# Samples' sums in four groups of eight rows up to the output, in a decoder layer with 32 experts

## The reference, cut to what matters

```python
h = h + mix
x = rmsnorm(h, norm_ffn)
gates, top_idx = softmax(top_k(x @ w_router + b_router, 4))
# per expert e: act = swiglu(x[rows] @ w_up[e] + b_up[e]); y = act @ w_down[e] + b_down[e]
h = h + einsum('tk,tkd->td', gates, y)
y_prompt, y_sample = rmsnorm(h[:256], norm_final), rmsnorm(h[256:], norm_final)
# rmsnorm(x, g) = x * rsqrt(mean(x * x) + 1e-6) * g
```

## Time and profile before

| | |
|---|---|
| median of three runs | 1089.74 us (1089.80, 1089.74, 1088.01) |
| the profiled execution, its own time | 1090.6 us |
| its span in the profile | 1088.8 us |
| busy in the span: PE, DVE, ACT, POOL | 1066.5, 361.5, 152.7, 12.1 us |
| moved by the DMA engines | 431.47 MB, 396 GB/s on average |
| granted clock of TensorE, mean | 0.995 |

### The profile page before, as it was taken

One profiled execution on the slowest core, in us unless ns is written; L12 is line 12 of the kernel. 1 busy time (PEld: TensorE's weight loads), 2 busy tenths in 40 slices (PEclk: granted clock), 3 DMA queues, 4 the chain that ended last, 5 costly groups with the idle time before them and its releaser, 6 DMA issues.

```text
span 1088.8 us, 13132 instructions
## 1 busy us (share of the span) xinstructions
PE 1066.5 (98%) x5662; PEld 446.4 (41%) x5663; DVE 361.5 (33%) x571; ACT 152.7 (14%) x302; POOL 12.1 (1%) x28
## 2 busy tenths in 40 slices
PE   8999999999999999999999999999999999999997
PEld 6888664333333333333333333333333333333332
DVE  3466534322222222222222222222332222232234
ACT  1121144111101111111111110111111011011113
POOL 1000000000000000000000000000000000000002
PEclk9999998999999999999999999999999999999999
DMA  9875948999999999999999999999999999999994
GB/s 293 305 266 205 393 170 329 407 428 430 433 427 434 427 430 433 432 429 431 428 434 430 429 435 426 432 428 432 433 430 433 428 430 434 422 427 427 427 409 172
DMA packets 40907, 431.47 MB, mean 396 GB/s; under 512 B 4456, under 2 KB 19852, under 8 KB 25104
## 3 DMA queue, kind: packets, MB, share of 16 engines
q1 hardware_dynamic: 40240, 430.41, 94.4%
q10 hardware_dynamic: 608, 0.20, 0.1%
HBM read 427.00 MB, written 3.48 MB: 395 GB/s over the span
## 4 chain that ended last, share of the span: by engine, by line
PE 80%; DMA 18%; DVE 0%; issue 0%; ACT 0%; POOLq 0%; DVEq 0%; POOL 0%; ACTq 0%
PE bank L999 35%; PE bank L1018 14%; DMA ring_all<-in_w_up 14%; PE bank L681 9%; PE bank L1063 5%; DMA ring_all<-in_w_down 4%; PE bank L973 4%; PE bank L1010 2%; PE bank L791 2%; PE bank L981 2%; PE bank L991 1%; PE bank L643 1%; PE bank L1056 1%; PE bank L1075 1%; PE bank L799 1%; PE bank L1101 1%
## 5 line engine op out<-in xcount | busy, mean ns | idle before, releaser
L999 PE MATMUL bank<-ring_all,work 128*64 128x512 f32 x2048 | 486.3, 602 | 7.9 <-DMA ring_all<-in_w_up 7.9
L999 PEld LDWEIGHTS bank<-ring_all,work 128*64 128x64 f32 x2048 | 135.0, 136 | 258.3 <-issue 248.8
L1018 PE MATMUL bank<-ring_all,work 128*64 128x512 f32 x992 | 225.3, 596 | 1.0 <-DMA ring_all<-in_w_down 1.0
L1827 DVE TENSOR_TENSOR h_tok<-h_tok,bank 128x1024 f32<-128x1024 f32 (+1 forms) x67 | 81.7, 1220 | 237.1 <-PE bank L1063 231.3
L1018 PEld LDWEIGHTS bank<-ring_all,work 128*64 128x64 f32 x992 | 68.5, 137 | 129.8 <-issue 128.8
L681 PE MATMUL bank<-work,ring_all 128*128 128x264 f32 x384 | 86.9, 387 | 0.0
L1797 DVE TENSOR_TENSOR work<-bank,bias_up 128x1024 f32<-128x1024 f32 x32 | 39.1, 1223 | 124.9 <-PE bank L1010 124.9
L681 PEld LDWEIGHTS bank<-work,ring_all 128*128 128x128 f32 x384 | 72.4, 190 | 12.4 <-DMA ring_all<-in_w_in 0.3
L1063 PE MATMUL bank<-work 64*128 64x512 f32 (+1 forms) x268 | 75.1, 637 | 0.0
L1814 DVE TENSOR_TENSOR work<-work 128x512 f32<-128x512 f32 x32 | 22.2, 692 | 108.6 <-ACT work L1403 108.5
L1387 ACT ACTIVATE work<-bank 128x264 f32<-128x264 f32 x32 | 12.5, 391 | 315.9 <-PE bank L991 315.9
(11 more groups left out here) (233 smaller groups left out, 546.3 us busy)
## 6 DMA issues: line engine op xcount, KB each, us to landing
ring_all<-in_w_up SPq DMA_DIRECT2D x48, 4096.0 KB, 33.2
ring_all<-in_w_down SPq DMA_DIRECT2D x24, 4096.0 KB, 34.2
ring_all<-in_w_up SPq DMA_DIRECT2D x30, 2048.0 KB, 37.9
ring_all<-in_w_down SPq DMA_DIRECT2D x13, 2048.0 KB, 39.8
ring_all<-in_w_in SPq DMA_DIRECT2D x13, 1024.0 KB, 5.1
ring_all<-in_w_down SPq DMA_DIRECT2D x6, 1024.0 KB, 22.0
ring_all<-in_w_out SPq DMA_DIRECT2D x4, 1024.0 KB, 11.8
ring_all<-in_w_up SPq DMA_DIRECT2D x4, 1024.0 KB, 5.8
```

The costliest lines, as they stand in the source:

```text
L999: mm = pe.matmul(bank[half * CAP:(half + 1) * CAP, up_bank(n) + b, :].rearrange("q (k p) -> q p k", k=KT), x, src[:, half * FF + b * 512:h ...
L1018: mm = pe.matmul(bank[half * CAP:(half + 1) * CAP, Y, :], av[:, 2 * i + k, :], src[:, k * D + half * 512:k * D + (half + 1) * 512], start= ...
L1827: tt(rows, rows, bank[0:m, b:b + 2, :], ALU.add).then_inc(comb_added, 1)
```

## The change

The samples' sums stay in the four groups of `sums` up to the output.

- All experts and the bias use the small pieces for c = 2. At expert 0, eight more products with the identity start the accumulation with the samples' rows of `h_tok`. The joining at expert 26 is gone.
- `sums` keeps its place, so norm_final moves into slot 6 of the ring (`late`), after chunk 186 of 192 has been used. SP loads, behind the last weights, a 0/1 matrix `same_row` (64 KB, row i and row j have a one where i and j are equal modulo 32), norm_final for the prompt, and norm_final once more for each of the four groups (`g_fold`): six transfers for one, with a semaphore of their own that POOL and PE wait for.
- The last combines, adds and squares of half 1 go in the order samples, tile 0, tile 1. For the samples they are over 128 partitions x 128 columns.
- The sums of squares of a sample's four groups are joined by two products of one column with `same_row` on PE, behind PE's register load and branch. DVE adds epsilon from PSUM, and POOL takes the samples' power together with tile 0's; tile 1 has its own.
- DVE scales tile 0, then all 256 columns of `sums` in one operation, then tile 1. ACT scales the two prompt tiles alone, and POOL multiplies two tiles where it did three.
- The samples are stored by four transfers of 8 rows x 2 pieces x 512 bytes, two issued by SP between the stores of tile 0 and tile 1, two by ACT behind its last row.

```diff
-            gt = lay(6304, T)[P - E:P]
-            g_fin = lay(5280, D)
+            gt = lay(6304, SEQ + 32)[P - E:P]
+            late = ring_all[:, LATE % RING, :]
+            g_fin = late[:, 0:D]
+            g_fold = late[:, D:D + 2 * P].rearrange("p (a b) -> p a b", a=2)
+            same_row = late[:, D + 2 * P:D + 3 * P]
-            weighted = [h_rows[:, 0:512], h_rows[:, 512:1024], xg[0:NS, :]]
+            weighted = [h_rows[:, 0:512], h_rows[:, 512:1024]]
...
-            FOLD = 26
+            LASTS = (2, 0, 1)
+            SCALE = (7, 6, 8)
...
+            last_sums = [(0, 0), (0, 1), (0, 2)] + [(1, c) for c in LASTS]
...
+            def y_folded(g):
+                return y_sample.rearrange("b s (n g t) -> g (b s) n t", n=2, g=4)[g]
...
-                sp.wait_ge(comb_psum, CT * (FOLD + 1))
+                sp.wait_ge(mm_done, LATE + 1)
+                sp.dma_start(same_row, c_square[:, 8, :]).then_inc(fin_in, 16)
                 sp.dma_start(g_fin[:], norm_final.rearrange("(a d) -> a d", a=1)
-                             .partition_broadcast(P)[:, 0, :]).then_inc(late_in, 16)
+                             .partition_broadcast(P)[:, 0, :]).then_inc(fin_in, 16)
+                for g in range(4):
+                    sp.dma_start(g_fold[32 * g:32 * g + NS], norm_final.rearrange("(a n g t) -> g a n t", a=1, n=2, g=4)[g]
+                                 .partition_broadcast(NS)[:, 0]).then_inc(fin_in, 16)
...
                 each_overflow(sp, greatest_load(sp), overflow)
-                for c in range(2):
-                    sp.wait_ge(fin_ready, c + 1)
-                    sp.wait_ge(fin_rows, c + 1)
-                    sp.dma_start(y_prompt[0, c * P:(c + 1) * P, :], h_tok[:, c, :]).then_inc(stored, 16)
+                sp.wait_ge(fin_ready, 1)
+                sp.wait_ge(fin_rows, 1)
+                sp.dma_start(y_prompt[0, 0:P, :], h_tok[:, 0, :]).then_inc(stored, 16)
+                sp.wait_ge(fin_ready, 2)
+                for g in range(2):
+                    sp.dma_start(y_folded(g), sums[32 * g:32 * g + NS]).then_inc(stored, 16)
                 sp.wait_ge(fin_ready, 3)
-                sp.wait_ge(fin_rows, 3)
-                sp.dma_start(y_sample.rearrange("b s d -> (b s) d"), h_tok[0:NS, 2, :]).then_inc(stored, 16)
-                sp.wait_ge(stored, 48)
+                sp.wait_ge(fin_rows, 2)
+                sp.dma_start(y_prompt[0, P:2 * P, :], h_tok[:, 1, :]).then_inc(stored, 16)
+                sp.wait_ge(stored, 96)
...
-                pool.wait_ge(late_in, 32)
-                for c in range(CT):
+                pool.wait_ge(fin_in, 96)
+                for c in range(2):
                     pool.wait_ge(comb_added, CT * (E - 1) + c + 1)
-                def last_root(c0, c1, i):
-                    pool.wait_ge(fin_ssq, c1)
-                    pool.tensor_tensor(st[:, 6 + c0:6 + c1], st[:, c0:c1], st[:, 3 + c0:3 + c1], ALU.add).then_inc(fin_chain, 1)
-                    pool.wait_ge(fin_chain, i + 1)
-                    pool.tensor_tensor(st[:, 6 + c0:6 + c1], st[:, 6 + c0:6 + c1],
-                                       minus_half[:].broadcast_to([P, c1 - c0]), ALU.pow).then_inc(fin_scale, 1)
-
-                pool.wait_ge(fin_eps, 1)
-                last_root(0, 1, 0)
-                last_root(1, CT, 1)
+                    pool.tensor_tensor(weighted[c], h_tok[:, c, 0:512], g_fin[:, 0:512], ALU.mult).then_inc(fin_weighted, 1)
+
+                def last_root(c, cols):
+                    at = SCALE[c]
+                    pool.tensor_tensor(st[:, at:at + 1], st[:, c:c + 1], st[:, 3 + c:4 + c], ALU.add).then_inc(fin_chain, 1)
+                    pool.wait_ge(fin_chain, c + 1)
+                    pool.tensor_tensor(st[:, at:at + cols], st[:, at:at + cols],
+                                       minus_half[:].broadcast_to([P, cols]), ALU.pow).then_inc(fin_scale, 1)
+
+                pool.wait_ge(fin_eps, 2)
+                pool.wait_ge(fin_ssq, 2)
+                last_root(0, 2)
+                pool.wait_ge(fin_ssq, 3)
+                last_root(1, 1)
...
-                    if c == 2 and isinstance(n, int) and n < FOLD:
+                    slot = n % 2 if isinstance(n, int) else 0
+                    if c == 2:
+                        if isinstance(n, int) and n == 0:
+                            for g in range(4):
+                                for half in range(2):
+                                    pe.matmul(bank[32 * g:32 * g + 32, C + half, 0:P], ident[0:NS, 0:32],
+                                              h_tok[0:NS, 2, half * 512 + g * P:half * 512 + (g + 1) * P], start=True, stop=False)
                         for g in range(4):
                             for half in range(2):
                                 at = slice(half * CAP, (half + 1) * CAP)
-                                mm = pe.matmul(bank[32 * g:32 * g + 32, C + half, 0:P], spread[at, n % 2, t0:t0 + 32],
-                                               y_rows[at, g * P:(g + 1) * P], start=True, stop=True)
+                                mm = pe.matmul(bank[32 * g:32 * g + 32, C + half, 0:P], spread[at, slot, t0:t0 + 32],
+                                               y_rows[at, g * P:(g + 1) * P], start=(not isinstance(n, int) or n > 0), stop=True)
                         mm.then_inc(comb_psum, 1)
                         return
-                    fold = c == 2 and isinstance(n, int) and n == FOLD
                     for half in range(2):
                         at = slice(half * CAP, (half + 1) * CAP)
-                        mm = pe.matmul(bank[0:m, at_bank + half, :], spread[at, n % 2 if isinstance(n, int) else 0, t0:t0 + m],
-                                       y_rows[at, :], start=True, stop=not fold)
-                    if fold:
-                        for half in range(2):
-                            for g in range(4):
-                                mm = pe.matmul(bank[0:m, C + half, g * P:(g + 1) * P], ident[:, 32 * g:32 * g + m],
-                                               sums[:, half, :], start=False, stop=(g == 3))
+                        mm = pe.matmul(bank[:, at_bank + half, :], spread[at, slot, t0:t0 + m],
+                                       y_rows[at, :], start=True, stop=True)
                     mm.then_inc(comb_psum, 1)
...
-                def combine_last(p, c):
-
+                def combine_last(i):
+
+                    p, c = last_sums[i]
                     t0, m = TOK[c]
-                    i = CT + CT * p + c
-                    pe.wait_ge(comb_added, CT * (E - 2) + i - 1)
-                    if c == 0:
+                    b = CL[(i + 1) % 2]
+                    pe.wait_ge(comb_added, CT * (E - 1) + i - 1)
+                    if i % CT == 0:
                         pe.wait_ge(y_copied, E + p)
                         pe.wait_ge(spread_copied, E)
-                    for half in range(2):
-                        at = slice(half * CAP, (half + 1) * CAP)
-                        mm = pe.matmul(bank[0:m, CL[i % 2] + half, 0:256], spread[at, (E - 1) % 2, t0:t0 + m],
-                                       y_rows[at, p * 256:(p + 1) * 256], start=True, stop=True)
+                    if c == 2:
+                        for g in (0, 2, 1, 3):
+                            at = slice(g // 2 * CAP, (g // 2 + 1) * CAP)
+                            mm = pe.matmul(bank[32 * g:32 * g + 32, b, 0:P], spread[at, (E - 1) % 2, t0:t0 + 32],
+                                           y_rows[at, p * 256 + g % 2 * P:p * 256 + (g % 2 + 1) * P], start=True, stop=True)
+                    else:
+                        for half in range(2):
+                            at = slice(half * CAP, (half + 1) * CAP)
+                            mm = pe.matmul(bank[:, b + half, 0:256], spread[at, (E - 1) % 2, t0:t0 + m],
+                                           y_rows[at, p * 256:(p + 1) * 256], start=True, stop=True)
                     mm.then_inc(comb_psum, 1)
...
-                                       start=True, stop=True)
+                        if c == 2:
+                            for g in range(4):
+                                mm = pe.matmul(bank[32 * g:32 * g + 32, C + half, 0:P], gt[:, t0:t0 + 32],
+                                               b_down_sb[:, half * 512 + g * P:half * 512 + (g + 1) * P], start=True, stop=True)
+                        else:
+                            mm = pe.matmul(bank[:, C + half, :], gt[:, t0:t0 + m], b_down_sb[:, half * 512:(half + 1) * 512],
...
                 each_overflow(pe, greatest_load(pe), overflow)
+                pe.wait_ge(fin_in, 96)
+                pe.wait_ge(fin_part, CT)
+                pe.wait_ge(fin_ssq, 1)
+                pe.matmul(bank[:, X, 0:1], same_row, st[:, 2:3], start=True, stop=False)
+                pe.matmul(bank[:, X, 0:1], same_row, st[:, 5:6], start=False, stop=True).then_inc(sel_psum, 1)
...
-                    n = TOK[c][1]
```

(66 more changed lines are left out.)

61 lines of the change are left out of this document (32 added, 29 removed).

## The result

| | before | after |
|---|---|---|
| median of ten runs | 1089.03 us (1088.01 to 1092.26) | 1092.72 us (1091.01 to 1094.22) |
| the profiled execution, its own time | 1090.6 us | 1091.75 us |
| its span | 1088.8 us | 1089.9 us |

The ratio is 1.0031, with a 95% interval from 1.0023 to 1.0039. The change costs about 3.4 us (2.5 to 4.2 by the interval). The forecast was no change, and the time lies above the range.

What follows compares the result with a forecast made beforehand. Up to 1058 us PE and the DMA transfers were taken as nearly equal streams, transfers landing last; time saved before counted 0, the tail's terms summed to +0.1 us on the 1089.74 median: forecast 1089.8, range 1087.9 to 1091.2.

Steps and rivals of the forecast that it cites:

- Steps (1) to (3): PE before 1058 us: eight more products (0.38), smaller bias product, small combines saving 4.16 us; all behind transfers, counted 0.
- rival A: PE is the bound up to 1058 us, so 4.16 us come through: 1085.6; chance 0.05, partial form 0.03.
- The named sign: Waits for ring_all grow by about 4 us between 952 and 1058, PE still passing its weights near 1058.
- Step (4): Samples' combine of expert 30 on PE, behind the last transfer PE waits for: 0.96 becomes 0.38, -0.58 us.
- Step (5): Last combines, adds and squares in the new order: squares end at 1081.9, chain 1.3 us shorter.
- Step (6): Samples' scale in series over PE, DVE, POOL behind PE's branch: first scale 0.2 us later (1082.8), second 0.7 earlier (1083.6).
- rival B: Late samples' path and SP's queue: 1090.7; with PE's code fetched, 1092 to 1093; fetch form shares 0.07 with late six transfers.
- The second scale: POOL's power for the second prompt block: 0.27 + 0.55 after the first scale, at 1083.6, 0.7 us earlier than before.
- Step (7): Scalings and stores: SP's two small stores at 0.69 us each, second block's store issued at 1085.5, before 1085.1.
- Step (8): End of the stores: SP's end at 1088.5, before 1088.4; sum +0.1 us, bounds -0.9 to +1.0.
- Step (9): Six transfers for the last norm land by 1075 to 1076; counted nothing, with 4 us of cover.
- Rival C: The six transfers land over 4 us late: +1 to +3 us; 0.07 together with the case of fetched branch code.

Runs made afterwards that it cites:

- e5: Kernel before with the joining of the groups at expert 29 instead of 26, tail untouched: 1089.69 us, ratio to before 1.0003.
- e2: Changed kernel with PE's branch turned round, so the usual case falls through into the selection products and then jumps: 1090.34 us, ratio to before 1.0008.
- e4: Changed kernel with SP storing the second prompt block ahead of its two small stores: 1093.8 us, ratio to before 1.0038.
- e1: Changed kernel with PE's selection products ahead of its register load and branch, leaving out the overflow case: 1090.21 us, ratio to before 1.0004.
- e8: Changed kernel with selection products ahead of the branch and DVE's first scaling held until POOL has both powers: tail 32.25 us, no ratio.
- e6: Changed kernel with branch turned, register load before the last down products, small stores spread over SP, ACT and POOL: 1089.46 us, ratio to before 1.0004.

## Why the prediction was wrong

- **Steps (1) to (3), counted at 0: right.** PE's busy time from 925 to 1058 fell by 3.9 us, of 4.16 named, and nothing came of it. e5 excludes rival A at its full price. The named sign, waits for ring_all, is there over the whole span: 10.4 us for w_up and 2.3 for w_down, before 7.9 and 1.0, so 3.8 more. From 952 to 1058 alone they are 2.7 us, against 0.16 before, where growth by 4 was forecast. The page's lines for the change, then for the kernel before:

```profile
L1018 PE MATMUL bank<-ring_all,work 128*64 128x512 f32 x2048 | 484.7, 600 | 10.5 <-DMA ring_all<-in_w_up 10.4
...
L1037 PE MATMUL bank<-ring_all,work 128*64 128x512 f32 x992 | 225.3, 596 | 2.3 <-DMA ring_all<-in_w_down 2.3
```

```profile
L999 PE MATMUL bank<-ring_all,work 128*64 128x512 f32 x2048 | 486.3, 602 | 7.9 <-DMA ring_all<-in_w_up 7.9
...
L1018 PE MATMUL bank<-ring_all,work 128*64 128x512 f32 x992 | 225.3, 596 | 1.0 <-DMA ring_all<-in_w_down 1.0
```

- **Step (4), -0.58: right.** From the anchor, the last copy of y starts after 19.96 us (1075.29 - 1055.33), before after 20.54 (1078.82 - 1058.28).
- **Step (5), the chain of squares: right within 0.2.** Forecast ends at 1081.9, that is 23.6 after the anchor; measured 1079.14 - 1055.33 = 23.8.
- **Step (6) failed: "the branch, at 1081.7 and 0.46 long, ended at 1082.2".** I took the old kernel's row over to the changed kernel, where the same branch is longer. The load began 21.3 after the anchor as forecast (1079.55 - 1058.28, measured 1076.6 - 1055.33). The branch took 3.78 for 0.46: **+3.3**. The products' way to DVE took 1.1 us (1082.51 minus the branch's end at 1081.38) where I took 0.6 at the bound: +0.5. Of this 0.4 goes with the granted clock, which fell to 0.50, the level of 1.2 GHz, while PE stood idle: its products take 0.56 each pair and DVE starts 1.02 us after the first, against 0.35 and 0.61 in e2 at 1.00. The fall need not have come by then: in e4, after the same 4.2 us of idling, the clock still stood at 1.00 and the first pair took 0.35. One window of the change shows its clock (columns as in the earlier trace rows):

```profile
1081.00:1083.00 2.00, 0.98 (x4) 0.93 (x4) 0.16 (x1) 0.00 (x0) 0.19 (x1) 0.50 0.03 8
```

  Both together are the 3.9 us by which POOL starts later than forecast: 1082.75 - 1055.33 = 27.4 after the anchor, not 1081.8 - 1058.28 = 23.5. The row of the kernel before did not hold for this kernel, and not for want of work behind the branch: e1, with nothing behind it either, shows 3.42. What made it cheap in the old form stays open. "An estimate from two to four of its 0.46 branches" in rival B named the cause with half the price or less, and at 0.07 with far too small a chance. That its total of 1092 to 1093 holds the measured 1092.72 is partly luck: it put 1.0 us on the late load and the small stores, where the tail has 0.55 beside the jump, and 1 to 2 on the jump, where the tail has 3.50. The sign in the rows was there: 459 ns on PE against 54 on ACT for the same instruction.
- **The second scale:** its power was put at 0.55 and took 0.96, beside DVE (e8): +0.4 on the second block alone.
- **Step (7), the stores:** two small ones on SP take 1.54, forecast 1.4. The two on ACT take 2.32, forecast 1.45 ("from 1084.45 to 1085.9"). Moving the large store ahead of them gains 0.38 with the branch in its place (e4), spreading them 1.16 once the branch is out of the way (e6 against e1).
- **Step (8), the sum +0.1:** the tail grew by 4.05. Without the jump it is e1's +0.55, inside the bounds -0.9 to +1.0 that the sum had for everything else: -0.61 from the new form itself (e6 against before) and +1.16 from its small stores. The range of 1087.9 to 1091.2 is narrower than bounds and spread together, which give 1087.1 to 1091.6; the measured time lies outside both.
- **Step (9), the six transfers: right.** POOL's first product starts at 1072.60, 17.3 after the anchor and 0.6 earlier than before (1076.13). Rival C did not occur. (The four small transfers carry 8 KB each, not 4: 8 rows of 256 values.)

## What to carry to other kernels

Before work is put behind a branch that jumps, price the jump in the changed program, on the engine at hand: the 0.46 us of the old program did not carry over, and the 50 to 72 ns of other engines did not either. Let the usual case fall through, or put the work ahead of the branch. PE was given 3.9 us less to do where it waits for transfers, and it was worth nothing. Where whole executions differ by 2 us, compare from an anchor in the trace, and repeat an execution before believing a rule.

## What the runs showed of the hardware

- A jump on PE over an unentered loop: 1.46 to 3.99 us in ten records, 3.0 or more in eight, and 0.37 and 0.46 in the two executions of the old form (e5 and before). With nothing but the program's end behind it, it takes 3.42 and 3.63 in the new form too (e1, e8). Where it falls through: 0.09. The same branch on SP, ACT and DVE: 50, 54 and 72 ns.
- Small stores of 8 rows in 2 pieces take 0.69 to 0.92 us to issue on SP, 0.73 to 1.55 on ACT, against 0.33 to 0.52 on SP for a block of 512 KB.
- POOL's one-column power: 0.55 us alone, 0.96 beside DVE's scaling.
- The part ahead of the tail varies with the clock in one place. Windows of the kernel before, and of the change:

```profile
166.00:173.00 7.00, 6.83 (x27) 2.45 (x23) 2.00 (x5) 1.93 (x4) 0.00 (x0) 0.55 0.66 282
```

```profile
166.00:173.00 7.00, 6.77 (x42) 3.44 (x42) 3.87 (x9) 2.89 (x5) 0.00 (x0) 1.00 0.82 321
```

  At a granted clock of 0.55 PE has 27 products there, at 1.00 it has 42. Among 14 profiled executions of 11 kernels, the four with 0.51 to 0.57 reach the anchor at 1057.1 to 1060.0, the four with 0.76 at 1057.0 to 1058.5, and the six with 1.00 at 1055.3 to 1058.1, four of them before 1056. The means are 1058.2, 1057.5 and 1056.2, so about 2 of the 2.95 us by which the change's profiled execution was ahead at the anchor go with this clock. It is not all of it: the two executions with 88 empty instructions both show 1.00 and reach the anchor at 1058.07 and 1055.65. The low level stands in the traces of old and new form, 1.00 only in those of the new. But among the 23 executions of the kernel before on the chip of e1, the six with a mean clock of 0.998 or 0.999 took 1087.8 us on average and the eleven with 0.994 or 0.995 took 1089.9, so the old form has both kinds as well, and the change need not be the reason. Why the clock stays up in some executions is open.
